# Turning the expert table u with transposing transfers on the sync queue instead of on TensorE

## The reference

```python
qry = (xb @ wq).reshape(blk, PEER_HEADS, 2, PEER_DHALF)
sc = jnp.einsum('thpd,hpkd->thpk', qry, subkeys)        # then top-16 of each half, top-16 of the sums
eid = e1 * PEER_NKEYS + e2                              # 128 picks of a token out of 16384 experts
g = jax.nn.softmax(sf, axis=-1)
ug = jnp.take(u_tab, eid, axis=0)
vg = jnp.take(v_tab, eid, axis=0)
act = jax.nn.gelu(jnp.einsum('td,thkd->thk', xb, ug))
return jnp.einsum('thk,thkd->td', (g * act), vg)
```

## Time and profile before

| | |
|---|---|
| median of 3 runs | 5693.61 us (5690.71 to 5696.09) |
| the profiled execution | 5688.19 us, its span 5686.5 us |
| TensorE busy (matmuls) | 4752.5 us, 84% of the span |
| VectorE busy | 2473.5 us, 43% |
| ScalarE busy | 1217.3 us, 21% |
| GpSimd busy | 1010.4 us, 18% |
| DMA moved | 628.50 MB |

### The profile page before, as it was taken

One profiled execution on the slowest core, in us unless ns is written; L12 is line 12 of the kernel. 1 busy time (PEld: TensorE's weight loads), 2 busy tenths in 40 slices (PEclk: granted clock), 3 DMA queues, 4 the chain that ended last, 5 costly groups with the idle time before them and its releaser, 6 DMA issues. The chain is left out here.

```text
span 5686.5 us, 77489 instructions
## 1 busy us (share of the span) xinstructions
PE 4752.5 (84%) x31089; PEld 2594.8 (46%) x31089; DVE 2473.5 (43%) x4385; ACT 1217.3 (21%) x1415; POOL 1010.4 (18%) x606
## 2 busy tenths in 40 slices
PE   6698756275377667989999999699999999999994
PEld 2354322263156335445555555344444544554542
DVE  4321000131376425058998994455545333333333
ACT  4200100131132322023444343111001111111113
POOL 0100000000032001000000000555555322222220
PEclk9799888556655787999999999899999999999997
DMA  6323222125210452126777776555555322222212
GB/s 237 111 87 108 107 90 88 66 63 140 68 37 26 163 170 74 52 99 146 169 162 163 162 160 138 153 150 149 147 146 146 99 69 69 73 68 73 69 50 72
DMA packets 1018359, 628.50 MB, mean 111 GB/s; under 512 B 854661, under 2 KB 920581, under 8 KB 1014314
## 3 DMA queue, kind: packets, MB, share of 16 engines
q1 hardware_dynamic: 446698, 503.26, 28.9%
q10 hardware_dynamic: 557600, 71.31, 8.2%
q0 software_dynamic: 13824, 50.51, 2.4%
HBM read 445.15 MB, written 210.54 MB: 115 GB/s over the span
## 5 line engine op out<-in xcount | busy, mean ns | idle before, releaser
L2412 PE MATMUL ex_psy<-ex_vhi,ex_whi 128*128 128x512 f16 x2048 | 777.0, 379 | 53.4 <-issue 53.2
L2412 PE MATMUL ex_psy<-ex_vlo,ex_whi 128*128 128x512 f16 x2048 | 776.9, 379 | 0.0
L2412 PE MATMUL ex_psy<-ex_vhi,ex_wlo 128*128 128x512 f16 x2048 | 776.7, 379 | 0.0
L2068 POOL TENSOR_SCALAR ex_v<-ex_v 128x1024 f32<-128x1024 f32 x128 | 365.3, 2854 | 2245.7 <-DMA ex_v<-in_peer_v_dram 2245.7
L2371 PE MATMUL ex_psa<-h_hi,ex_uth 128*128 128x512 f16 (+1 forms) x3072 | 641.2, 318 | 9.0 <-ACT ex_wa L2097 9.0
L2371 PE MATMUL ex_psa<-h_lo,ex_uth 128*128 128x512 f16 (+1 forms) x3072 | 640.7, 317 | 0.0
L2371 PE MATMUL ex_psa<-h_hi,ex_utl 128*128 128x512 f16 (+1 forms) x3072 | 640.7, 317 | 0.0
L2339 DVE TENSOR_TENSOR ex_acc<-ex_acc,ex_psy 128x512 f32<-128x512 f32 x496 | 332.9, 684 | 465.3 <-PE ex_psy L2412 464.5
L2326 DVE SCALAR_TENSOR_TENSOR ex_wa<-ex_wa,ex_gate 128x1088 f32<-128x1088 f32 x128 | 173.9, 1358 | 464.2 <-ACT ex_wa L2097 424.6
L2371 PEld LDWEIGHTS ex_psa<-h_lo,ex_uth 128*128 128x128 f16 x3072 | 229.7, 98 | 243.0 <-issue 1.1
L2371 PEld LDWEIGHTS ex_psa<-h_hi,ex_uth 128*128 128x128 f16 x3072 | 234.7, 98 | 231.9 <-issue 12.9
(11 more groups left out here) (341 smaller groups left out, 7427.4 us busy)
## 6 DMA issues: line engine op xcount, KB each, us to landing
gate_all<-rt_stage ACTq DMA_DIRECT2D x34, 2048.0 KB, 19.3
ex_gate<-gate_all SPq DMA_DIRECT2D x128, 544.0 KB, 6.6
ex_u<-in_peer_u_dram SPq DMA_DIRECT2D x128, 512.0 KB, 3.5
ex_v<-in_peer_v_dram SPq DMA_DIRECT2D x128, 512.0 KB
act_all<-ex_wa SPq DMA_DIRECT2D x80, 544.0 KB
ex_wa<-act_all SPq DMA_DIRECT2D x80, 544.0 KB, 4.9
adw<-in_ada_w_dram SPq DMA_DIRECT2D x12, 2048.0 KB
pn_w<-in_w_in_dram SPq DMA_DIRECT2D x8, 1664.0 KB, 7.0
```

The lines of the kernel that those rows point to most:

```text
L2068: nc.gpsimd.tensor_scalar(v[:, :], v[:, :], SPLIT, None, ALU.mult).then_inc(v_sc, 1)
L2412: mm = nc.tensor.matmul(out, x, y, start=(j == 0), stop=(j == len(mms) - 1))
```

## The change

The 16 transposes on TensorE, the two PSUM tiles, the identity tile and both evacuations are gone. In their place SyncE issues two transposing transfers for each block, from `u_hi[s]` and `u_lo[s]` straight to `ut_h[s]` and `ut_l[s]`, both in SBUF. The products wait for them to land, and so does the `split` that writes `u_hi[s]` next.

```diff
+                def turn(eb, s):
+                    sp.wait_ge(u_lo_done, eb + 3)
+                    if not (isinstance(eb, int) and eb < 2):
+                        sp.wait_ge(acted, eb + 1)
+                    sp.sem_inc(turn_clear, 1)
+                    for dst, src in ((ut_h, u_hi), (ut_l, u_lo)):
+                        sp.dma_start_transpose(dst[s][:, :, :], src[s][:, :, :].rearrange("p k d -> p (k d)")).then_inc(ut_in[s], 16)
...
                 load_u(1, 1)
+                turn(0, 0)
                 for eb in range(AHEAD):
                     load_u(eb + 2, eb % 2)
+                    turn(eb + 1, (eb + 1) % 2)
                     if eb % PER_SLOT == 5 and eb // PER_SLOT < PT:
                         load_scores(eb // PER_SLOT + 1)
...
-                        elif more(eb, 2):
-                            load_u(eb + 2, s)
+                        else:
+                            if more(eb, 2):
+                                load_u(eb + 2, s)
+                            if more(eb, 1):
+                                turn(eb + 1, 1 - s)
...
                 def split(eb, s):
                     act.wait_ge(u_in[s], (eb - s) * 8 + 16)
-                    act.wait_ge(u_tr, eb + 1)
+                    if not (isinstance(eb, int) and eb < 2):
+                        act.wait_ge(ut_in[s], (eb - s) * 16)
...
-                def turned(eb, s):
-                    act.wait_ge(u_tr, eb + 3)
-                    act.wait_ge(acted, eb + 1)
-                    nc.scalar.copy(ut_h[s][:, :, :], ps_t[0][:, :, :]).then_inc(ut_hi, 1)
...
-                def turned(eb, s):
-                    dve.wait_ge(u_tr, eb + 3)
-                    dve.wait_ge(acted, eb + 1)
-                    V.tensor_copy(ut_l[s][:, :, :], ps_t[1][:, :, :]).then_inc(ut_lo, 1)
...
-                def turn(eb, s):
...
-                    for part, src in enumerate((u_hi, u_lo)):
-                        for k in range(KD):
-                            mm = nc.tensor.transpose(ps_t[part][:, k, :], src[s][:, k, :], ident[:, :])
-                    mm.then_inc(u_tr, 1)
...
                     if ks[0] == 0:
-                        pe.wait_ge(ut_hi, eb + 1)
-                        pe.wait_ge(ut_lo, eb + 1)
+                        pe.wait_ge(ut_in[s], (eb - s) * 16 + 32)
                         pe.wait_ge(gelu_done, eb + 1)
```

More of the change, by code:

```diff
@@ L1931, in experts @@
     two = lambda name: [pr.sem(f"ex_{name}{s}") for s in range(2)]
-    u_in, g_in, wa_in, wa_stored = two("uin"), two("gin"), two("wain"), two("wastored")
+    u_in, ut_in, g_in, wa_in, wa_stored = two("uin"), two("utin"), two("gin"), two("wain"), two("wastored")
     v_in = pr.sem("ex_vin")
-    (u_hi_done, u_lo_done, u_tr, ut_hi, ut_lo, acted, gelu_done, w_done, w_hi_done, w_lo_done, v_sc, v_hi_done, v_lo_done,
+    (u_hi_done, u_lo_done, acted, gelu_done, w_done, w_hi_done, w_lo_done, v_sc, v_hi_done, v_lo_done,
      y_done, added, ready, passed) = (pr.sem(f"ex_{n}") for n in (
-         "uhi", "ulo", "utr", "uthi", "utlo", "acted", "gelu", "w", "whi", "wlo", "vsc", "vhi", "vlo", "y", "added", "ready",
+         "uhi", "ulo", "acted", "gelu", "w", "whi", "wlo", "vsc", "vhi", "vlo", "y", "added", "ready",
          "passed"))
@@ L1942, in experts @@
     stage_stored = [pr.sem(f"sg_stored{s}") for s in range(2)]
+    turn_clear = pr.sem("ex_turnclear")
     act_all = t["act_all"]
@@ L1975, in experts @@
             w_hi, w_lo = ([sb(f"{n}{s}", [P, TOK], F16) for s in range(2 * EB)] for n in ("whi", "wlo"))
-            ident = sb("ident", [P, P], F16)
             u = [sb(f"u{s}", [P, D]) for s in range(2)]
@@ L1981, in experts @@
             ps_a = late.enter_context(nc.psum_tensor("ex_psa", [P, 3 * 512], F32))
-            ps_t = [late.enter_context(nc.psum_tensor(f"ex_pst{s}", [P, KD, P], F16)) for s in range(2)]
             with ExitStack() as early:
@@ L2127, in _ @@
                 split(1, 1)
-                turned(0, 0)
                 for n in range(SLOTS):
@@ L2131, in _ @@
                         eb = n * PER_SLOT + j
-                        turned(eb + 1, (eb + 1) % 2)
                         split(eb + 2, eb % 2)
@@ L2147, in half @@
                         if not is_kept(g1, kept):
-                            if more(eb, 1):
-                                turned(eb + 1, 1 - s)
                             if more(eb, 2):
@@ L2166, in _ @@
                 STEPS = 23
-                V.tensor_copy(ident[:, :], pr.c("ident")).then_inc(ready, 1)
                 V.tensor_copy(iota_h[:, :, :], pr.c("iota128").unsqueeze(2).broadcast_to([P, KEYS, INNER])).then_inc(ready, 1)
                 V.tensor_copy(ranks[:, :, :], pr.c("iota16").unsqueeze(2).broadcast_to([P, TOPK, TOPK])).then_inc(ready, 1)
-                dve.wait_ge(ready, 3)
+                dve.wait_ge(ready, 2)
                 dve.sem_inc(u_lo_done, 2)
@@ L2344, in _ @@
             def _(pe):
-                pe.wait_ge(ready, 3)
-                pe.sem_inc(u_tr, 2)
+                pe.wait_ge(ready, 2)
                 pe.sem_inc(acted, 2)
-                def turn(eb, s):
[L2351 to L2355, removed]
-                    for part, src in enumerate((u_hi, u_lo)):
-                        for k in range(KD):
-                            mm = nc.tensor.transpose(ps_t[part][:, k, :], src[s][:, k, :], ident[:, :])
-                    mm.then_inc(u_tr, 1)
                 def products(eb, s, ks):
                     if ks[0] == 0:
-                        pe.wait_ge(ut_hi, eb + 1)
-                        pe.wait_ge(ut_lo, eb + 1)
+                        pe.wait_ge(ut_in[s], (eb - s) * 16 + 32)
                         pe.wait_ge(gelu_done, eb + 1)
@@ L2413, in unit @@
                     mm.then_inc(y_done, 1)
-                turn(0, 0)
                 for n in range(SLOTS):
@@ L2420, in _ @@
                         eb = n * PER_SLOT + j
-                        turn(eb + 1, (eb + 1) % 2)
                         products(eb, eb % 2, range(0, 4))
@@ L2430, in half @@
                             eb = g1 * EB + b
-                            if more(eb, 1):
-                                turn(eb + 1, 1 - b % 2)
                             products(eb, b % 2, range(KD))
```

## The result

The changed kernel takes 5711.31 us in the median of 7 runs (5703.51 to 5714.89), the kernel before 5693.61 us in the median of 7 (5690.34 to 5701.38) on the same chip: a ratio of 1.0029, 95% interval 1.0017 to 1.0041. It is slower by 18 us where 43 us less were forecast. The profiled execution has a span of 5706.2 us, 19.7 us above that of before.

What follows compares the result with a forecast made beforehand. The prediction took TensorE to bound the kernel in AHEAD and Late. It summed -42 - 22 + 19 + 2 = -43 us against the profiled 5688.2 to 5645, so 5650 us as median; forecast's own range 5620 to 5675, overall 5610 to 6000.

Steps and rivals of the forecast that it cites:

- What bounds the kernel; what TensorE saves: TensorE at its limit in AHEAD and Late; dropping the turn saves 42 us in Late, 22 in AHEAD, where gelu is late next.
- What a pair of transposing transfers costs: SyncE's two transfers for a block: 5.5 us from issue to landing of both, with 3.5 and 19.3 as ends.
- X: Time from SyncE's issue of the pair to the landing of both transfers, taken as 5.5 us.
- Who waits for the pair: SyncE's queue in AHEAD: activation store behind the pair hidden up to X = 8.8; 19 us lost in 8 iterations loading scores.
- A: In AHEAD, the end of the products of block eb-1, when the pair for block eb+1 is issued.
- the first rival: SyncE's queue in AHEAD: stores of activations wait behind the pair, slower, 5831 us at X = 14, 6053 at 19.3; chance 0.22.
- Scores: AHEAD, 8 iterations: load of scores between pair and store makes the store land 2.4 us late, 19 us in all.
- The second rival: AHEAD, where gates are stored: DMA engines are full, slower, 5943 us at 8 us of engine time a pair; chance 0.16.
- both of its signs: Full DMA engines would show as store of gates landing much later than 19.3 us and a DMA share near 1.
- my limit of 3.4: AHEAD: up to 3.4 us of all 16 DMA engines for a pair fit into an iteration at no cost.
- The first block: Start of the kernel: the pair plus a handover takes 6 to 7 us for 4.9 before, +2 us.
- The sum: Whole kernel: -42 - 22 + 19 + 2 = -43 us against the profiled 5688.2.

Runs made afterwards that it cites:

- e1: Changed kernel, but in AHEAD SyncE issues the load of scores and the store of the activation ahead of the pair; 5630.51 us, 0.9892 of the kernel before.
- e5: e1, but in AHEAD TensorE turns the high half of u by 8 transposes and one transfer the low half; 5636.81 us, 0.9906 of the kernel before.
- e6: e1, but in AHEAD gelu runs in two parts and the next block's first three products wait for the first alone; 5592.11 us, 0.9825 of before.
- e9: Kernel with transposing transfers in Late alone, plus 16 unread transposes before every second group's first products in Late; 5657.52 us, 0.9935 of the kernel before.
- e7: Changed kernel, but the load of scores goes out ahead of the pair, the activation's store stays behind it; 5674.93 us, 0.9969 of the kernel before.
- e3: Changed kernel in its own order, but each store of gates writes only a quarter of its rows; 5634.18 us, 0.9902 of the kernel before.

## Why the prediction was wrong, point by point

- **What bounds the kernel; what TensorE saves.** Right. AHEAD's iterations of 13.46 us (in e1) and Late's saving of 0.9 us an iteration are in the table, and gelu as what is late next was shown by e5 and e6: the gap of 1.49 us was to become 0.98 when gelu's first part is enough, and is 1.01. In e1 AHEAD saves 20 us for the 22 forecast. Late's 42 us came out as 34: 1 us because one of the 47 turns falls ahead of Late's first gelu, and 7 in the four long iterations, which I put down to the clock behind the pauses (e9). The prediction did not weigh that; it is argued from rows, and e9 did not settle it.
- **What a pair of transposing transfers costs.** This is the step that failed. The prediction takes one X = 5.5 us for every pair; that holds where the DMA engines are free, with 4.65 at the first block. I had taken it from the landing of u, 3.5 us over the whole span and in AHEAD alone too, and so put what a store of gates beside the pair does at nothing, though u had landed beside such stores only in the old mix. In the changed kernel the load of u itself lands in 8.7 us in AHEAD, and X is 13.0 in the iteration shown, over the 9 us at which the prediction called itself wrong altogether. The Trainium skill, page VectorE: DVE Perf Modes, section The three transpose paths, gives 1309 ns for one tile; by an estimate 16 of them in a row would be 21 us, and no pair here is as slow. By the page DMA: Bandwidth & Descriptors of the Trainium skill, section Latency and other measured facts, 261 GB/s would be an estimate of 2.0 us for the pair; not even one transfer of the two landed in under 3.0 us here, so the pages bound the pair no closer than the rows did.
- **Who waits for the pair.** The place was right: the store behind the pair on SyncE, and gelu behind the store. The rule for it was not. The prediction lets the store go out when the pair has landed, at A + X + 0.4; it goes out when the pair has been issued, at A + 6.74 with X at 13.0. And it was to land 4.5 us after its issue, where gelu waits 9.1 (2923.70 to 2932.77). With the rule as written, X = 13.0 gives gelu at A + 17.9; it is A + 15.8. So the first rival, which I gave 0.22, is what happened in some 28 of the 80 iterations, at a smaller price than at X = 14, partly for that reason and partly because not every pair is slow. Scores: 19 us forecast, 45 measured against e1, of which e7 takes away 33.
- **The second rival**, full DMA engines, is wrong as a lack of engine time, and my rule for it with it, though both of its signs came near: a DMA share of 0.91 and stores of gates that land in 22.3 us for 19.3. Full queues did matter, by making every landing later (e3). The pair costs the engines more than I allowed: queue q1 of SyncE holds 48.0% in the changed kernel from 2900 to 3300 us, for 23.7% before, which is 7.0 us for an iteration and 3.3 before:

```profile
q10 hardware_dynamic: 219270, 28.04, 48.0%
q1 hardware_dynamic: 65520, 47.59, 48.0%
```

  So the pair takes 3.7 us of all engines, over my limit of 3.4. Yet e1 runs at a share of 1.00 and e6 at 1.08 with no iteration lengthened by a store.
- **The first block.** +2 us forecast; from the end of the first low half of u to the first product it is 4.65 us for 4.9 before, and nothing was lost.
- **The sum.** -43 forecast. With the store in its right place the same change gives -60 (e1), so the terms of the gain, 64 us in all, were about right, and the late stores cost 78 us on top.

## What to carry to other kernels

When a transfer is put into a queue, work out the deadline of every transfer behind it with the landing times that they will have in the new mix, not those of the old trace: here one line further up in the queue was worth 80 us. Where two transfers of one iteration compete for a place, the one that is wanted sooner goes first, and a store that frees a buffer is as urgent as a load. And when work is taken from an engine, look at what that work had been covering: TensorE's turn had covered gelu, and splitting gelu in two gave another 38 us.

## What the runs showed of the hardware that was not expected

- A transposing transfer of 128 x 1024 16-bit elements from SBUF to SBUF lands in 3.0 to 3.3 us when little else moves and, in the changed kernel, in up to 11.1 us beside a store in 128-byte runs; SyncE is held 1.23 to 1.4 us by its issue at best and there up to 4.7 us.
- It goes in small packets: SyncE's queue has 270336 packets and 67.1 MB more than before for 256 transfers, so 1056 packets and 262144 bytes each.
- A DMA share of 1.00 in the profile is not a full machine. In AHEAD it was 0.91 at 181 GB/s in the changed kernel, where transfers were late, and 1.00 at 193 in e1, where gelu waited for no store. E6, over 2449 to 3400 us, shows more than one:

```profile
2449.00:3400.00 951.00, 936.56 (x7346) 514.40 (x7344) 822.88 (x2380) 336.80 (x393) 0.00 (x0) 1.00 1.08 201
```

- After pauses of 3.0 to 3.6 us TensorE's clock went to half at some times and stayed at others.
